# Weighting and adding one token tile's expert rows on ScalarE and GpSimd instead of VectorE

## The reference

```python
def hier_moe(x, w_group, w_router, w_gate, w_up, w_down):
    ...
    e_top, e_idx = lax.top_k(e_logits, TOP_K_INNER)
    e_w = jax.nn.softmax(e_top, axis=-1) * g_w
    expert_id = (g_sel[:, None] * EXPERTS_PER_GROUP + e_idx).reshape(-1)
    token_id = jnp.repeat(jnp.arange(n_tok), TOP_K_INNER)
    weight = e_w.reshape(-1)
    ...
    def expert_block(args):
        xblk, e = args
        hid = jax.nn.silu(xblk @ w_gate[e]) * (xblk @ w_up[e])
        return hid @ w_down[e]

    yb = lax.map(expert_block, (xb, blk_expert)).reshape(n_rows, dm)
    y = jnp.zeros_like(xt).at[row_token].add(yb * row_weight[:, None].astype(yb.dtype))
    return y.reshape(bsz, seq, dm)

def reference(x, ...):
    for i in range(DEPTH):
        h = rms_norm(x, attn_norm[i])
        if i % 2 == 0:
            x = x + even_mixer(h, ...)
        else:
            x = x + odd_mixer(h, ...)
        h = rms_norm(x, ffn_norm[i])
        x = x + hier_moe(h, moe_router_group[i], moe_router_expert[i], moe_w_gate[i], moe_w_up[i], moe_w_down[i])
    return x
```

## Time and profile before

| | us |
|---|---|
| median of 3 runs | 1660.56 |
| lowest and highest of them | 1660.13, 1665.9 |
| the profiled execution's own time | 1665.72 |
| its span in the trace | 1663.7 |
| PE busy | 1596.9 (96%) |
| DVE busy | 487.0 (29%) |
| ACT busy | 357.2 (21%) |
| POOL busy | 197.6 (12%) |

### The profile page before, as it was taken

The page is one execution under the profiler, slowest core; times in us unless marked ns, Lnnn a source line. Parts: engine busy times, 40 slices in busy tenths (PEclk is TensorE's granted clock), DMA queues, the critical chain, the costliest instruction groups (busy, mean ns, idle before and its releaser), DMA issues.

```text
span 1663.7 us, 21206 instructions
## 1 busy us (share of the span) xinstructions
PE 1596.9 (96%) x8028; PEld 752.1 (45%) x8028; DVE 487.0 (29%) x1252; ACT 357.2 (21%) x837; POOL 197.6 (12%) x298
## 2 busy tenths in 40 slices
PE   7999899999999999999899989999999999999995
PEld 4545574543333333333445457865433333333332
DVE  1485751541111111111412235643511111111114
ACT  2354451311111111111200236642111110111110
POOL 2240320000000000000101012320000000000000
PEclk9999999999999999999999999999999999999999
DMA  8620127289999999999924220033699999999997
GB/s 240 253 101 7 55 51 303 83 331 420 422 422 421 422 422 422 422 422 412 347 30 147 94 54 1 2 161 143 259 422 422 421 422 422 422 422 422 422 421 315
DMA packets 118312, 474.20 MB, mean 285 GB/s; under 512 B 40821, under 2 KB 47221, under 8 KB 68332
## 3 DMA queue, kind: packets, MB, share of 16 engines
q1 hardware_dynamic: 110156, 456.98, 68.6%
q10 hardware_dynamic: 3136, 8.40, 1.3%
q0 software_dynamic: 4960, 8.04, 1.3%
HBM read 454.84 MB, written 26.77 MB: 289 GB/s over the span
## 4 chain that ended last, share of the span: by engine, by line
PE 77%; SPq 12%; DMA 4%; DVE 4%; issue 2%; ACT 1%; POOL 1%; DVEq 0%; ACTq 0%; POOLq 0%
PE bank L1857 19%; SPq L1803 10%; PE bank L1870 9%; PE bank L1475 8%; PE bank L1830 8%; PE bank L550 7%; PE bank L844 6%; PE bank L438 4%; DMA arena<-in_moe_w_up 3%; PE bank L403 3%; PE bank L1845 2%; SPq L1812 2%; PE bank L420 2%; PE bank L925 2%; PE bank L1863 1%
## 5 line engine op out<-in xcount | busy, mean ns | idle before, releaser
L1857 PE MATMUL bank<-arena 128*64 128x512 f32 x2048 | 451.8, 593 | 5.9 <-DMA arena<-in_moe_w_up 5.7
L1857 PEld LDWEIGHTS bank<-arena 128*64 128x64 f32 x2048 | 143.7, 137 | 302.3 <-issue 291.5
L1870 PE MATMUL bank<-arena 128*64 128x512 f32 x1024 | 230.6, 592 | 2.1 <-DVE arena L1963 2.1
L1959 DVE TENSOR_TENSOR arena<-arena,bank 128x256 f32<-128x256 f32 x64 | 26.9, 421 | 640.8 <-ACT arena L1949 640.8
L1876 POOL DMA_INDIRECT y_d<-arena,slot_row x62 | 60.7, 979 | 861.8 <-ACT arena L1954 834.7
L1830 PE MATMUL bank<-arena 128*64 128x512 bf16 x1280 | 161.3, 381 | 1.0 <-DVE arena L718 0.8
L1475 PE MATMUL bank<-arena 128*128 128x512 f32 x320 | 138.4, 593 | 0.8 <-ACT arena L320 0.8
L1870 PEld LDWEIGHTS bank<-arena 128*64 128x64 f32 x1024 | 71.9, 137 | 124.1 <-issue 110.5
L550 PE MATMUL bank<-arena 128*128 128x512 f32 x256 | 113.6, 601 | 0.0
L1949 ACT ACTIVATE arena<-bank 128x256 f32<-128x256 f32 x64 | 24.5, 383 | 411.6 <-PE bank L1857 411.6
L844 PE MATMUL bank<-arena 128*128 128x512 f32 (+1 forms) x288 | 106.9, 531 | 0.0
(11 more groups left out here) (310 smaller groups left out, 1461.2 us busy)
## 6 DMA issues: line engine op xcount, KB each, us to landing
arena<-in_moe_w_gate SPq DMA_DIRECT2D x128, 1024.0 KB, 20.0
arena<-in_moe_w_up SPq DMA_DIRECT2D x128, 1024.0 KB, 22.9
arena<-in_moe_w_down SPq DMA_DIRECT2D x62, 2048.0 KB, 23.3
arena<-in_even_w_in SPq DMA_DIRECT2D x4, 2048.0 KB, 8.3
y_d<-arena ACTq DMA_DIRECT2D x2, 4096.0 KB, 16.7
arena<-y_d SPq DMA_DIRECT2D x8, 1024.0 KB, 9.4
arena<-bias_row_d SPq DMA_DIRECT2D x2, 3584.0 KB, 11.2
arena<-in_odd_w_in SPq DMA_DIRECT2D x3, 2048.0 KB, 8.3
```

Source lines behind the costliest of these rows:

```text
L1857: mm = nc.tensor.matmul(bank[1][fh * CAP:(fh + 1) * CAP, :], xeT[:, j, half * CAP:(half + 1) * CAP], wgu[u][:, :, n, fh * FH:(fh + 1) * FH ...
L1870: mm = nc.tensor.matmul(bank[3][dh * CAP:(dh + 1) * CAP, :], hidT[:, j, fh * CAP:(fh + 1) * CAP], wd[u][:, n, dh * 512:(dh + 1) * 512], st ...
```

## The change

One tile of four, tile 1 (`POOL_TILE = 1`), is taken out of DVE's `add_fetched`. ACT multiplies its two fetched rows by `other_w` in place (two ACTIVATE of 128x1024 that copy with a scale), and POOL adds each product to `xt` (two TENSOR_TENSOR of 128x1024). ACT waits for DVE's weights (`other`) and for the transfer of tile 1 (`m_yin1`). POOL waits for each product (`pool_w`) and for its own additions (`pool_add`). DVE waits for the second addition (`pool_add`) ahead of `add_last(1)`. The order on DVE changes too: `add_last(0)` now stands straight behind `add_fetched(0)`, and tile 1's and tile 2's `add_last` stand together behind `add_fetched(2)`. This is done in both layers.

```diff
--- before.py
+++ after.py
@@ -156,7 +156,7 @@
     "oq_turned": ("qk_turned", 5), "oss": ("ssq", 5), "oss_ms": ("ssq_ms", 5), "oss_rstd": ("ssq_rstd", 5),
     "qscale": ("hgain", 1),
 
-    "m_rw": ("bias_out", 16), "m_rmm": ("bias_mm", 2), "m_oh": ("conv", 8),
+    "other": ("dt_ln", 1), "pool_w": ("kn", 2), "pool_add": ("dt_exp", 1), "m_rw": ("bias_out", 16), "m_rmm": ("bias_mm", 2), "m_oh": ("conv", 8),
     "zeros": ("pads", 1), "y_zero": ("acol_in", 32), "m_fin": ("yd_mm", 4), "m_lturn": ("st_mm", 3), "m_lT": ("sq", 5),
     "m_lones": ("y_gated", 4), "mx0_yin": ("brow", 2), "mx1_yin": ("relb_ones", 1),
     "m_cnt": ("ix_mm", 12), "m_routed": ("selm", 3), 
@@ -2007,6 +2007,8 @@
                     eng.nop()
             eng.nop()
 
+        POOL_TILE = 1
+
         def moe_sp(sp, L, mixed, att):
             t, x = "m", f"mx{L}"
             if L == 0:
@@ -2209,7 +2211,12 @@
                 x_step(act, x, j, X_DN)
                 nc.scalar.activation(yb[:, 0, :], bank[3][:, :], ACT.Copy).then_inc(S(f"{x}_step"), 1)
 
-            further(act, t, L, more)
+            further(act, t, L, more, last=lambda n: act.wait_ge(S(f"{x}_yin"), past(f"{x}_yin") + 16 * NT))
+            act.wait_ge(S("other"), past("other") + L + 1)
+            act.wait_ge(S(f"{t}_yin{POOL_TILE}"), 16 * (L + 1))
+            for k in range(2):
+                y_ = y_rows[:, k, POOL_TILE, :]
+                nc.scalar.activation(y_, y_, ACT.Copy, scale=other_w[:, k, POOL_TILE:POOL_TILE + 1]).then_inc(S("pool_w"), 1)
 
         def moe_pool(pool, L):
             t, x = "m", f"mx{L}"
@@ -2229,6 +2236,11 @@
                 pool.wait_ge(S(f"{x}_yout"), 16 * (j + 1))
                 pool.sem_inc(S(f"{x}_step"), 1)
             further(pool, t, L, more)
+            xs = xt[:, POOL_TILE, :]
+            for k in range(2):
+                pool.wait_ge(S("pool_w"), past("pool_w") + 2 * L + k + 1)
+                nc.gpsimd.tensor_tensor(xs, xs, y_rows[:, k, POOL_TILE, :], ALU.add).then_inc(S("pool_add"), 1)
+                pool.wait_ge(S("pool_add"), past("pool_add") + 2 * L + k + 1)
             pool.wait_ge(S("m_fin"), past("m_fin") + NT * (L + 1))
             pool.sem_inc(S(f"{t}_yfree"), 1)
 
@@ -2328,6 +2340,7 @@
                 link(v_.tensor_scalar(keep, shifted, float((NE + 1) * CAP), None, ALU.is_ge))
                 link(v_.tensor_tensor(keep, keep, low, ALU.add))
                 link(v_.tensor_tensor(flat(other_w[:]), keep, flat(weight[:]), ALU.mult))
+                dve.sem_inc(S("other"), 1)
 
             def body(e, c, cu, u, after):
                 opening = isinstance(c, int) and c == L * NE
@@ -2381,10 +2394,13 @@
                     xs = xt[:, i, h * 512:(h + 1) * 512]
                     v_.tensor_tensor(xs, xs, bank[2 * i + h][:, :], ALU.add).then_inc(S(f"{t}_x"), 1)
             add_fetched(0)
-            for i in range(1, NT):
+            add_last(0)
+            for i in range(POOL_TILE + 1, NT):
                 add_fetched(i)
-                add_last(i - 1)
-            add_last(NT - 1)
+                if i == POOL_TILE + 1:
+                    dve.wait_ge(S("pool_add"), past("pool_add") + 2 * L + 2)
+                    add_last(POOL_TILE)
+                add_last(i)
 
 
         block = ctx.enter_context(nc.Block())
```

## The result

| | before | changed |
|---|---|---|
| median, us | 1661.39 (22 runs) | 1665.0 (22 runs) |
| lowest and highest, us | 1657.8, 1665.9 | 1660.97, 1671.17 |
| ratio to before | | 1.0019, 95% interval 1.001 to 1.0028 |

The kernel became slower by 0.19%, or 3.2 us, with 1.7 to 4.7 inside the interval (the two medians in the table differ by 3.6). The forecast was +2.3 us (1662.9 on the first three runs' median). The direction held and the time lies in the range; the interval holds both the forecast and more than it.

A forecast was written before the change was run, and what follows sets the result against it. PE was taken to bound the kernel, with DVE on the chain only at the hand-over and the end. +1.4 us at the end and +0.9 at the hand-over made +2.3, so 1662.9 us; range 1658.3 to 1669.0.

The forecast's parts named there:

- The bound and the two places: PE holds 77% of the chain; the change matters only at layer 1's end and the hand-over from layer 0.
- The end of layer 1: From the last fetch's first issue to DVE's last addition: claimed 1.4 us later, all on the path to the end.
- POOL's addition: Each of POOL's two 128x1024 additions for tile 1 was to take 2.39 us, within bounds 1.83 and 2.54.
- a held multiply-add: DVE's 1024-wide multiply-add on tile 2, waiting for POOL's addition, was to end 1.08 us after POOL lets go.
- POOL after DVE: POOL's second addition, waiting for DVE's multiply-add on tile 2, was to take 2.24 us from there.
- ACT's scaled copy: Each of ACT's two 128x1024 scaled copies of tile 1 was to take 1.05 us, adding 0 to the end.
- the wait for PE: `add_last(0)`, now behind one pair, was to wait for PE's last expert products, losing 1.1 us of the gain.
- the wait for tile 2's landing and the holding: DVE at tile 2, held until POOL's additions are through: claimed +2.9 us.
- ACT's branch: Between ACT's start of `yb` and its first copy: between 0 and 2.06 us, taken as 1.1.
- The norm at the hand-over: In layer 0, POOL's norm steps queue behind its additions, so the last square on ACT starts 0.9 us later.
- The clock: Rival, chance 0.18: PE's waits at the hand-over halve its clock for 6.8 us, costing at most 3.4 more.
- Side by side: Rival, chance 0.17: POOL and DVE don't hold each other at either place; together -2.2 us, 1658.4.

The follow-up runs named there:

- only_l1: The change made in layer 1 alone, layer 0 left as in the kernel before; 1.0013 of the kernel before.
- one_sbuf: The changed kernel, but DVE weights tiles 2 and 3 into their PSUM banks, leaving it one SBUF input; 0.9981 and 0.9988 of the kernel before.
- pe_awake: The changed kernel with six instead of three idle-time matmuls on PE ahead of the norm's; 1.0024 of the kernel before, hand-over 30.43 us.
- both_ways: Layer 0 as in one_sbuf; in layer 1 no POOL additions, PE adds tile 3's fetched rows through diagonal matrices; 0.9997 of the kernel before.
- only_l0: The change made in layer 0 alone, layer 1 left as in the kernel before; 1.0015 of the kernel before.
- after_again: The changed kernel run once more, with nothing altered; 1.0025 of the kernel before.
- pe_adds: Against the kernel before: PE, not DVE, weights and adds tiles 2 and 3's fetched rows through diagonal matrices, without POOL additions; 1.0008 of it.

## Why the prediction was right

**The bound and the two places.** Right. The cost appears at the hand-over and at the end, and each half alone shows its own part.

**The end of layer 1.** +1.4 was forecast, +1.36 in the profile, +1.22 in only_l1. The terms: POOL's addition 2.39 forecast, 2.36 measured; a held multiply-add 1.08 after POOL's end, 1.09 and 1.10 measured; POOL after DVE 2.24, 2.19 measured. Small terms were off against each other: ACT's scaled copy takes 1.13 to 1.15 us, not 1.05, and the wait for PE is 0.8 to 1.0 us, not 1.1, while the wait for tile 2's landing and the holding come to 0.71 + 2.55 = 3.3 us, not 2.9. ACT's branch was taken as 1.1 us behind the start of `yb`; the copy started 1.02 behind it (794.63 and 795.65 us in the changed profile), and the landing of tile 1 ended the wait, so there was nothing late.

**The norm at the hand-over.** Here a term of the sum was mis-sized: +0.9 was forecast, +3.0 measured. It has two parts. The last square, L268, starts 811.84 - 786.89 = 24.95 us after the issue, against 22.87 before: +2.1 instead of +0.9. I let the sum's L276 run free at 0.22 us and only the power L278 be held, and that by one multiply-add. In fact both are held, one behind each of tile 3's two multiply-adds, 1.20 and 1.58 us, so the second diagonal starts at 809.10, behind the end of the pair at 808.64. In the kernel before L276 was never held, and I took that over without asking where it fell between DVE's instructions: it started 0.03 to 0.04 us behind the start of a multiply-add there (804.71 against 804.67, 808.56 against 808.53) and ran in 0.22, but 0.16 us behind one in the changed kernel (806.20 against 806.04). one_sbuf shows the cause: with DVE's second SBUF input gone L276 takes 0.22 us and L278 0.57, and the last square starts 21.4 us after the issue.

**The clock.** The other 0.9 us of the hand-over. I had it as a rival with 0.18 and priced it at up to 3.4. The fall was there, by the sign that the prediction gave for it, and for longer than the rows showed (10.2 us against 6.8), but it cost 0.9, as pe_awake shows. For much of it PE would have waited for ACT and POOL anyway: in pe_awake it waits again ahead of each tile's 16 matmuls. In the changed kernel the last 48 run without a break from 809.55 to 817.39, so when the last diagonal is ready (813.97 + 0.40 = 814.37) PE is still at work on the tile before. The clock is full again by then, and what is left of the fall is this backlog: PE is done 3.02 us after the diagonal, in pe_awake 2.10. So the forecast and this rival were both partly true: they don't exclude each other, and PE's long wait, which I had worked out as 2.7 us (3.00 measured), leads from the one to the other.

**Side by side.** Refuted by the changed profile's 1.63 and 3.25 us for the two multiply-adds, and by one_sbuf, which is what this rival would have been: it forecast -2.2 us, and one_sbuf's stretches give -1.84.

**The times.** +2.3 forecast, +3.2 measured (1.7 to 4.7), +4.36 in the stretches. The stretches say that the sum was 2.1 us too low, all of it at the hand-over (1.2 for the held L276 and L278, 0.9 for the clock). That the time came nearer than that is in part luck: the profiled execution won back 1.15 us where nothing was changed. The whole is 0.19%, and the forecast of no change beyond 0.5% held with room, since the two stretches together are 50 us of 1660.

## What to carry to other kernels

Before work is moved from DVE to POOL, look for what both read: if DVE's instructions beside it have two SBUF inputs, the times add up instead of overlapping, and POOL's smallest steps (here a one-column norm that the next stage waits for) are held until the DVE instruction is done. With one of DVE's inputs in PSUM the same move paid here (one_sbuf). A queue that gets new work also delays everything behind it, old waits included; price the first instruction behind it, not only the one moved, and look at the end of the queue too: here POOL's closing DRAIN made a version 1.2 us longer behind its last useful instruction.

## What the runs showed of the hardware that I had not expected

- A POOL instruction on one column is held as long as an addition of 1024: L276 took 0.94 and 1.20 us instead of 0.22 (+0.7 and +1.0), the addition 3.20 instead of 2.36 (+0.8).
- A multiply-add on DVE that reads one PSUM operand and writes PSUM costs 0.75 us for 512 columns, the same as the SBUF one, and leaves POOL alone.
- Fp32 matmul passes of 512 columns took 7.13 / 16 = 0.45 us each with 128 rows, and 3.7 / 16 = 0.23 us with 64 rows, on the upper and the lower half of the rows in turn: there they start in pairs, 0.01 to 0.04 us apart (799.82 and 799.85 us in before).
- With a wait of PE of 2.24 to 3.00 us came a stretch at 1.2 GHz in both_ways (end) and in the changed kernel, only_l0 and after_again (hand-over), for 3.4 to 10.2 us. In pe_awake a wait of 2.65 us, behind more work, was not.
- POOL's closing DRAIN took 5.14 us in every kernel looked at here; it was hidden behind DVE's work except in pe_adds and both_ways.
